# A hybrid decoder layer on one core: where the down weights' copies are made

## What is computed

```python
def conv_ffn(hn, w_up, conv_w, conv_b, w_down):
    u = causal_dwconv(hn @ w_up.astype(hn.dtype), conv_w) + conv_b.astype(hn.dtype)
    a, b = jnp.split(u, 2, axis=-1)
    return (jax.nn.silu(a) * b) @ w_down.astype(hn.dtype)      # w_down: 2816 x 1024

for layer in range(DEPTH):
    h = h + mixer_block(rmsnorm(h, norm1[layer]), ...)
    h = h + conv_ffn(rmsnorm(h, norm2[layer]), ...)
```

## Time and profile before

| | us |
|---|---|
| median of 3 runs | 1974.22 |
| the runs | 1975.3, 1974.22, 1974.14 |
| span of the profiled execution, first to last instruction | 1972.5 |
| TensorE busy in it | 1940.7 |
| VectorE busy | 1289.1 |
| ScalarE busy | 793.8 |
| GpSimd busy | 331.9 |

### The profile page before, as it was taken

The page is one execution under the profiler, slowest core; times in us unless marked ns, Lnnn a source line. Parts: engine busy times, 40 slices in busy tenths (PEclk is TensorE's granted clock), DMA queues, the critical chain, the costliest instruction groups (busy, mean ns, idle before and its releaser), DMA issues.

```text
span 1972.5 us, 32168 instructions
## 1 busy us (share of the span) xinstructions
PE 1940.7 (98%) x13188; PEld 1874.7 (95%) x13188; DVE 1289.1 (65%) x1612; ACT 793.8 (40%) x1095; POOL 331.9 (17%) x327
## 2 busy tenths in 40 slices
PE   8999999999999989999999999999999999999998
PEld 7999998999999989999999999999999999988887
DVE  6456664747576667667633433278988889866666
ACT  5123332534333444445443333234444443445443
POOL 0000001577474122222200100200000000000001
PEclk9999999999999999999999999999999999999999
DMA  9665567654555574646436552322433545578664
GB/s 294 215 206 140 127 166 197 187 174 161 172 182 156 119 186 148 170 153 184 142 109 175 155 152 77 105 66 74 129 107 107 145 146 166 154 246 278 192 192 160
DMA packets 301223, 316.39 MB, mean 160 GB/s; under 512 B 151004, under 2 KB 220996, under 8 KB 300948
## 3 DMA queue, kind: packets, MB, share of 16 engines
q1 hardware_dynamic: 291860, 291.25, 48.2%
q0 software_dynamic: 9216, 23.07, 5.9%
HBM read 223.16 MB, written 114.18 MB: 171 GB/s over the span
## 4 chain that ended last, share of the span: by engine, by line
PE 89%; DVE 4%; DMA 3%; ACT 1%; issue 1%; SPq 1%; POOL 0%; DVEq 0%; POOLq 0%; ACTq 0%
PE a_psum L1148 35%; PE a_psum L1431 18%; PE a_psum L155 10%; PE a_psum L1441 10%; PE a_psum L1135 5%; PE a_psum L1223 1%; DMA w_raw<-in_w_in 1%; PE a_psum L1242 1%; PE a_psum L1328 1%; PE a_psum L1252 1%; PE a_psum L1205 1%; PE a_psum L1312 1%; PE a_psum L1220 1%; PE a_psum L1268 1%; PE a_psum L1343 1%
## 5 line engine op out<-in xcount | busy, mean ns | idle before, releaser
L1148 PE MATMUL a_psum<-xh,w_hi 128*128 128x342 f32 (+3 forms) x1656 | 537.2, 324 | 6.8 <-DVE w_lo L1894 6.8
L1148 PE MATMUL a_psum<-xl,w_hi 128*128 128x342 f32 (+3 forms) x1656 | 532.2, 321 | 0.0
L1148 PE MATMUL a_psum<-xh,w_lo 128*128 128x342 f32 (+3 forms) x1656 | 530.4, 320 | 0.0
L1148 PEld LDWEIGHTS a_psum<-xh,w_hi 128*128 128x128 f32 x1656 | 312.9, 189 | 9.3 <-DVE w_lo L1894 7.9
L1148 PEld LDWEIGHTS a_psum<-xl,w_hi 128*128 128x128 f32 x1656 | 313.1, 189 | 0.6
L1148 PEld LDWEIGHTS a_psum<-xh,w_lo 128*128 128x128 f32 x1656 | 312.9, 189 | 0.0
L1586 ACT ACTIVATE post<-a_psum 128x342 f32<-128x342 f32 (+3 forms) x207 | 94.5, 457 | 513.2 <-PE a_psum L1148 483.6
L1894 DVE TENSOR_TENSOR w_lo<-w_raw,w_hi 128x1024 fp32r<-128x1024 f32 x87 | 113.2, 1301 | 144.8 <-ACT w_hi L1511 144.8
L1511 ACT ACTIVATE w_hi<-w_raw 128x1024 fp32r<-128x1024 f32 x87 | 91.6, 1053 | 112.0 <-PE a_psum L155 64.0
L1431 PE MATMUL a_psum<-x_t_hi,up_hi 128*128 128x258 f32 x608 | 123.5, 284 | 2.7 <-DVE post L2367 2.5
L1441 PE MATMUL a_psum<-act_hi,down_hi 128*128 128x512 f32 (+1 forms) x324 | 123.6, 382 | 1.7 <-DVE act_lo L2420 1.6
(11 more groups left out here) (289 smaller groups left out, 3953.0 us busy)
## 6 DMA issues: line engine op xcount, KB each, us to landing
w_raw<-in_w_in SPq DMA_DIRECT2D x76, 512.0 KB, 3.9
up_raw<-in_w_up SPq DMA_DIRECT2D x19, 1024.0 KB, 4.9
mix_scratch<-post SPq DMA_DIRECT2D x32, 522.0 KB, 3.0
down_sums<-in_w_ffn_down POOLq DMA_DIRECT2D x4, 2816.0 KB, 30.4
act_scratch<-post SPq DMA_DIRECT2D x22, 512.0 KB, 2.7
down_raw<-down_sums SPq DMA_DIRECT2D x44, 256.0 KB, 2.7
act_raw<-act_sums SPq DMA_DIRECT2D x44, 256.0 KB, 3.2
ext<-mix_scratch SPq DMA_DIRECT2D x9, 1024.0 KB, 7.1
```

The source lines that it names most:

```text
L1148: mm = pe.matmul(psum[:, u % 2, 0:n], w[:, k, :], x[:, k, at0:at0 + n], start=(k == 0 and part == 0), stop=(k == KC - 1 and part == 2))
```

## The change

The four copies of 1408 x 512 are gone from ahead of unit (5, 0). In their place, ahead of each of the first 44 of the 48 units of tiles 49 to 64, POOL waits until `units_done` counts every unit before it, and issues one copy of 128 x 512. The later waits on `w_sums` count 44 copies in place of 4. No other line changes.

```diff
             def load_down(q):
                 p, k = q // KH, q % KH
                 if q == KH:
-                    sp.wait_ge(w_sums, 16 * (4 + 3 * KH))
+                    sp.wait_ge(w_sums, 16 * (4 * KH + 3 * KH))
                 elif q == 5 * KH:
-                    sp.wait_ge(w_sums, 16 * (4 + 4 * KH))
+                    sp.wait_ge(w_sums, 16 * (4 * KH + 4 * KH))
...
-            ws = [sc["ws"][n].rearrange("k p c -> (k p) c") for n in range(4)]
...
-                if kind == "proj" and a == (5, 0):
-                    pool.wait_ge(units_done, tiles_done(4))
-                    for into, of in zip(ws, (a21, a11, a11, a12)):
-                        pool.dma_start(into, of).then_inc(w_sums, 16)
+                if kind == "proj" and T_ZB <= a[0] < T_ZA and 3 * (a[0] - T_ZB) + a[1] < 4 * KH:
+                    u = 3 * (a[0] - T_ZB) + a[1]
+                    n, k = u // KH, u % KH
+                    pool.wait_ge(units_done, 3 * a[0] + a[1])
+                    pool.dma_start(sc["ws"][n, k], (a21, a11, a11, a12)[n][k * P:k * P + P, :]).then_inc(w_sums, 16)
                 elif kind == "proj" and a[0] >= T_ZA and (3 * (a[0] - T_ZA) + a[1]) % 2 and 3 * (a[0] - T_ZA) + a[1] < 4 * KH:
                     k = (3 * (a[0] - T_ZA) + a[1]) // 2
                     pool.wait_ge(units_done, 3 * a[0] + a[1])
-                    pool.wait_ge(w_sums, 64)
+                    pool.wait_ge(w_sums, 16 * 4 * KH)
...
                 if j % KH == 0:
-                    pool.wait_ge(w_sums, 16 * (4 + 2 * KH + j))
+                    pool.wait_ge(w_sums, 16 * (4 * KH + 2 * KH + j))
```

## The result

The changed kernel takes **1980.87 us** (median of 6 runs, 1977.75 to 1983.34), the kernel before 1974.4 us on the same chip (6 runs, 1970.44 to 1975.58). The ratio is 1.0035, with a 95% interval of 1.0026 to 1.0045: **slower by 0.35%**, about 6.5 us, where the forecast was no difference and the range ended at 1978.9 us.

What follows compares the result with a forecast made beforehand. TensorE, busy 1940.7 of 1972.5 us, was taken as the bound. Minus 1.3, plus 2.7, minus 0.2 gave plus 1.2 us on 1974.22: 1975.4 us, called no difference, range 1972.4 to 1978.9.

Steps and rivals of the forecast that it cites:

- What it adds: four waits ahead of each `expand`: In the chunks, the products of `expand` run one unit later but are read two units after that: price 0.
- the 3.9 us taken as the least that a measurement can tell: For the whole kernel, about 0.2% or 3.9 us was the smallest difference a measurement could tell from no change.
- The VectorE rival: In eight chunks, a POOL issue of 0.8 us lengthens VectorE's work, which TensorE awaits: 1981.8 us, chance 0.03.
- Three copies in front of the load of `w_raw`: At the start of the gate tiles, three blocks delay a load that TensorE already waits for: plus 2.7 us.
- The early gain: Between 70 and 120 us, two short TensorE waits behind the four large copies go: minus 1.3 us, at most that.
- Minus 0.2 us for L2239: In the chunks, a product no longer beside VectorE's L2239 saves 0.2 us, between 0 and 0.4.
- The other 41 transfers and the 44 issues: In the chunks, copies one to a unit fit the query load's margin, and POOL covers issues of 0.81 us: price 0.
- the bound of 2 us: Over all chunks, the upper bound on what the other 41 transfers could cost, 0 to 2 us.

Runs made afterwards that it cites:

- e10: Changed kernel, with wait and issue of the seven copies directly ahead of `expand` put behind its products, the other 37 copies unmoved: 1980.63 us.
- e13: Kernel before, with the first `expand` product given the second's wait so both run back to back, no copies or unit waits added: 1974.9 us.
- e14: Changed kernel, with the first product of each `expand` issued right behind the `qk` work, ahead of the four waits, the second behind them: 1976.66 us.
- e1: The changed kernel run again, unaltered, for a second profile: 1981.28 us.
- e2: Changed kernel, with all copies of a chunk and their waits put behind the chunk's `expand`, in gate units 6 to 41: 1978.12 us.
- e15: e14 without copies in gate units 0 to 6; the 44 are made in units 7 to 47, the last three units two each: 1973.47 us.
- e12: Changed kernel without copies in gate units 0 to 6; the 44 are made in units 7 to 47, the last three units two each: 1977.73 us.
- e6: Kernel before, with its large copies, plus seven block copies in gate units 0 to 6: 1976.7 us.
- e9: Kernel before, plus the 44 waits and seven transfers of 256 KB, one directly ahead of each `expand`: 1974.75 us.
- e3: Kernel before, with its four large copies, plus the 44 waits on POOL and no block copies: 1975.21 us.
- e5: e2 without copies in gate units 0 to 6; the 44 are made in units 7 to 47, the last three units two each: 1975.15 us.
- e11: e10 without copies in gate units 0 to 6; the 44 are made in units 7 to 47, the last three two at a time: 1977.93 us.
- e7: Changed kernel, with the wait for the seven copies directly ahead of `expand` kept there but their issues moved behind it: 1976.3 us.

## Why the prediction was wrong

**The step that failed is "What it adds: four waits ahead of each `expand`", its "Price 0 on the path".** I looked at who reads the products, found two units to spare, and left it there. That part is true: no one waits for a product. I did see that a product slows a VectorE operation beside it, and allowed "the same 0.9 us" at the new place. Two things were missed. The step makes two products, and rows 9 show the second alone (x1, at 818.54 us); once POOL is late for the first too, they stand back to back and a held operation takes 3.0 us more, not 0.9. And I did not ask who waits for the held operation at the new place: behind L2109 stand `w_lo` and L2223, for which TensorE waits at once. It isn't that the new place is worse as such: in e10 the pair runs 5.6 us earlier in the chunk, ahead of the old place, and the fourth chunk loses 3.7 us there; in e13, 1.1 us after that, it loses nothing. The price is about 4.75 us in each of two profiles, where the term had 0; e14, which undoes this and nothing else, lowers the median by 4.2 us against the first set of runs and 4.6 against e1.

The range ended at 1978.9 us, a number that no sum of the prediction gives (its own bound, 3.9 us above 1974.2, is 1978.1); the measured time lies above both. A smaller step failed with it: the 3.9 us taken as the least that a measurement can tell. The interval measured here is 1.9 us to either side.

**The VectorE rival** had the right victim and the wrong culprit. It made the issues lengthen VectorE's work, and gave 1981.8 us, close to the result by luck, for a reason that isn't the one: e2, e14 and e15 keep the 44 issues (0.53 us each) without the loss. I gave it 0.03. The page it drew on (the Trainium skill, SBUF — State Buffer, "SBUF: two separate sides") also states that a VectorE operation with two SBUF inputs contends with GpSimd operations that read SBUF, and that the loser blocks for the whole instruction. The products of `expand` are such operations, an issue is none: by that statement the products had to be priced, and the rival turned it on the issues alone. The measured 4.23 us agree with it, for two instructions in a row instead of one; that a shared port is the reason is the page's account, and no run here shows more than the durations. The page's other statement, that whichever starts first gets the ports, is not what the recorded starts show (last section).

**Three copies in front of the load of `w_raw`, plus 2.7 us: right in size and place.** The load was to land in about 9 us (8.2 to 9.7 measured, 6.2 to 6.6 without) and the wait to be 7 to 8 us. It is 6.8 on average, 2.3 us above the average without copies. e15 against e14 is 3.2 us in the medians, e12 against e1 3.2 when each is taken against the kernel before beside it, and e6 against before is 3.0. The count of three was nearly so: four copies are issued before the load lands, in the first profile the fourth 2.5 us ahead of it. The first profile alone, with its 5.2 us, would have said that this term was wrong.

**The early gain, minus 1.3 us: right.** All profiles can be compared here, by the time from the unit at 70 us to the one at 179 us. In the twelve profiles without large copies it is the same to 0.01 us, 1.78 us shorter than in the first profile of before. In the four experiments that keep the large copies it is 0.09, 0.60, 1.29 and 1.63 us shorter (e9, e13, e3, e6), so what these copies cost changes from one execution to the next, between 0.15 and 1.8 us, 1.1 on the mean of five. The bound "the gain can't be above that" was half a microsecond too low.

**Minus 0.2 us for L2239** was right to a tenth: with the second product gone from beside L2239 and no pair, the chunk is 34.13 instead of 34.35 us (e14, e15).

**The other 41 transfers and the 44 issues, price 0: right,** for copies that come one to a unit. An issue holds POOL for 0.53 us, not 0.81. e5, with three at once, lost 1.8 us in one chunk, near the bound of 2 us.

**Sum as measured:** plus 4.75 for the chunks (0 in the forecast), plus 2.3 to 3.2 for the gate start (2.7), minus 1.1 for the early tiles (1.3): 6.0 to 6.9 us, and the medians give 6.5.

## What to carry to other kernels

A wait put ahead of an instruction does not only make it late: it can push together what ran apart. Where GpSimd and VectorE work side by side, list for each moved GpSimd operation what VectorE runs at the new time, and who waits behind it, not only who reads the moved result. And look for the one load that TensorE already waits for before putting any transfer in front of it; here the first few blocks of 256 KB cost 2 to 3 us at that load, and the others, one to a unit in the chunks, nothing that could be told.

## What the runs showed of the hardware that I had not expected

- A VectorE product of two SBUF operands (1.22 us alone) was held for both of two back-to-back GpSimd products (2.95 us) and took 4.13 to 4.27 us, in the changed kernel, e1, e10, e11 and e12. It did not get its turn between them. In e3 and e7, where the pair is on record 0.3 to 0.6 us ahead of it, it took 2.84 us, and the pair over 4.
- The recorded start does not say who wins. L2109 is on record 0.18 us ahead of the pair and is held for 4.23 us; L2239 in e13, 0.08 us ahead of the pair, runs in 1.23 us, and the same line in the fifth chunk of the changed kernel, also 0.08 us ahead (859.45 and 859.53), takes 4.13; L2109 in e9, 0.54 us ahead, runs in 1.22. What decides is open.
- A third to half a microsecond on POOL decided 2 to 3 us of TensorE: the pair at 21.26 us costs 1.15 us in the fourth chunk, at 21.8 us 3.3, and at 22.13 us 0.4.
- Issues of DMAs from GpSimd did not lengthen VectorE's work anywhere that I looked: in e14 L2106 (825.62 us) and L2229 (819.95 us) take 1.23 and 1.22 us, as ever, with an issue of 0.53 us during each (826.53 and 820.96 us).
- SP's issue of one and the same query load (L921, at the gate start) held its queue for 0.49 to 2.17 us in the seventeen profiles. In the two profiles of the changed kernel it was 0.49 and 1.37 us, and the longest wait of TensorE 5.2 and 6.4. What sets it is open.
